# Rotary sums on all partitions, and the heads' blocks laid side by side by ScalarE copies, in a two-layer hybrid encoder step

## What is computed

```
hn = rmsnorm(x); proj = hn @ w_in
def rotary(x, pos):            # x: (B, L, heads, 64)
    x1, x2 = x[..., :32], x[..., 32:]
    return concatenate([x1 * cos - x2 * sin, x1 * sin + x2 * cos], axis=-1)
qa = rotary(heads(qa), pos)
ka = rotary(heads(ka), pos) * scale
A = retention(qa, ka, va)      # 4 heads, chunks of 64 frames
B = gated linear attention     # 4 heads, chunks of 64 frames
C = band attention             # 8 heads
x = x + concat[A, B, C] @ w_out
x = x + relu(rmsnorm(x) @ w_up)**2 @ w_down
```

## Time and profile before

| | |
|---|---|
| time before, median of 3 runs (from, to) | 1419.89 us (1417.8, 1420.12) |
| the profiled execution | 1420.84 us |
| its span, first to last instruction | 1419.0 us |
| granted TensorE clock, mean over the span | 0.991 |

### The profile page before, as it was taken

How to read it: one execution, slowest core, us unless ns; L and a number is a source line. 1 busy time by engine, 2 the same in 40 slices (tenths; PEclk the granted TensorE clock), 3 DMA queues, 4 the chain that set the end, 5 groups by cost and what they waited for, 6 DMA issues and landing times. The chain is left out here.

```text
span 1419.0 us, 28637 instructions
## 1 busy us (share of the span) xinstructions
PE 1386.3 (98%) x12590; PEld 1344.8 (95%) x12590; DVE 776.7 (55%) x1224; ACT 521.3 (37%) x859; POOL 147.1 (10%) x107
## 2 busy tenths in 40 slices
PE   8999999999999999999999999999999999999996
PEld 8899898899999999999998998989999999999996
DVE  6897767745434334344768967675453343433433
ACT  5333556633223223123433345565331231322331
POOL 0200000031110110200202000001301102002012
PEclk9999999999999999999999999999999999999997
DMA  6113333222222222222221224422222222222211
GB/s 230 61 65 100 95 118 95 78 102 90 88 81 87 89 90 90 90 90 89 77 75 46 67 88 132 134 74 77 88 90 90 90 90 90 85 82 88 89 61 63
DMA packets 50635, 127.82 MB, mean 90 GB/s; under 512 B 8400, under 2 KB 17744, under 8 KB 50512
## 3 DMA queue, kind: packets, MB, share of 16 engines
q1 hardware_dynamic: 50224, 125.44, 26.7%
q10 hardware_dynamic: 288, 0.55, 0.1%
HBM read 118.77 MB, written 7.21 MB: 89 GB/s over the span
## 5 line engine op out<-in xcount | busy, mean ns | idle before, releaser
L1302 PE MATMUL PS<-xhi,whi 128*128 128x272 f32 x1920 | 565.0, 294 | 4.0 <-DVE wlo L767 3.1
L1302 PE MATMUL PS<-xhi,wlo 128*128 128x272 f32 x1920 | 557.2, 290 | 0.0
L1302 PE MATMUL PS<-xlo,whi 128*128 128x272 f32 x1920 | 554.8, 289 | 0.0
L767 DVE TENSOR_TENSOR wlo<-raw,whi 128x1024 fp32r<-128x1024 f32 x200 | 252.9, 1264 | 386.1 <-ACT whi L467 385.3
L467 ACT ACTIVATE whi<-raw 128x1024 fp32r<-128x1024 f32 x200 | 211.5, 1059 | 548.4 <-PE PS L1302 543.9
L1302 PEld LDWEIGHTS PS<-xhi,whi 128*128 128x128 f32 x1920 | 363.2, 189 | 15.5 <-issue 9.7
L1302 PE MATMUL PS<-zhi,wlo 128*128 128x272 f32 x1280 | 371.0, 290 | 0.0
L1302 PE MATMUL PS<-zhi,whi 128*128 128x272 f32 x1280 | 368.8, 288 | 0.4 <-DVE wlo L767 0.4
L1302 PE MATMUL PS<-zlo,whi 128*128 128x272 f32 x1280 | 368.7, 288 | 0.0
L1302 PEld LDWEIGHTS PS<-xlo,whi 128*128 128x128 f32 x1920 | 363.8, 189 | 0.2
L1302 PEld LDWEIGHTS PS<-xhi,wlo 128*128 128x128 f32 x1920 | 363.3, 189 | 0.0
(11 more groups left out here) (226 smaller groups left out, 1050.3 us busy)
## 6 DMA issues: line engine op xcount, KB each, us to landing
raw<-in_wu SPq DMA_DIRECT2D x199, 512.0 KB, 3.4
Bh<-in_bias SPq DMA_DIRECT2D x16, 256.0 KB, 4.1
h<-in_x SPq DMA_DIRECT2D x8, 272.0 KB, 6.1
out_k_t<-att_k SPq DMA_DIRECT2D x8, 272.0 KB, 4.4
out_y_t<-y SPq DMA_DIRECT2D x8, 272.0 KB, 2.7
kct<-in_ck SPq DMA_DIRECT2D x8, 256.0 KB, 3.1
cvb<-in_cv SPq DMA_DIRECT2D x8, 256.0 KB, 4.7
out_v_p<-vtk SPq DMA_DIRECT2D x8, 256.0 KB, 2.2
```

What stands on the lines that cost most here:

```text
L767: nc.vector.tensor_tensor(wlo[n % SPL][:, :], raw[n % RAW][:, :], f32(whi[n % SPL][:, :]), ALU.subtract).then_inc(sems["w_lo"], 1)
L1302: return nc.tensor.matmul(out, lhsT, rhs, start=start, stop=stop, skip_group_check=True)
```

## The change

`rotary` becomes two DVE operations on all 128 partitions: the difference goes to the tile `r2`, the sum to `ssum` (both are free at this time). They are announced on a new semaphore, `rot_sum`. A new step of ACT, `"apart"`, then copies four blocks of 32x544 at a time from `r2` and `ssum` to their places in `rk` or `rq`, and raises `rot_ready`. It stands at the end of the ACT steps of slots (8, 1), (9, 0), (10, 1) and (11, 0). DVE's sums of q wait for the copies of k (`rot_ready` 2), since they use the same two tiles. In a run this takes away 32 DVE operations of 32x544 and adds 8 of 128x544 and 32 ACT copies of 32x544. The semaphore's entries in the lists of counts and names are left out here.

```diff
--- before.py
+++ after.py
@@ -73,7 +73,9 @@
     _steps[(12, 0)] = _steps[(12, 0)] + [("gn", GLA)]
     _steps[(15, 0)] = [("gn", RET)]
 GN_PARTS = [(0, 8), (8, 20)]
-ROTARY = {(8, 0): (RK, 0), (8, 1): (RK, 1), (10, 0): (RQ, 0), (10, 1): (RQ, 1)}
+ROTARY = {(8, 0): RK, (10, 0): RQ}
+for _slot, _first, _g in (((8, 1), RK, 0), ((9, 0), RK, 1), ((10, 1), RQ, 0), ((11, 0), RQ, 1)):
+    ACT_STEPS[_slot] = ACT_STEPS.get(_slot, []) + [("apart", _first, _g)]
 for _u in range(4):
     _b = 16 + 3 * _u
     DVE_STEPS[(_b + 1, 0)] = [("norm", _u, 0), ("score", _u, 1)]
@@ -565,6 +567,18 @@
                                 nc.scalar.activation(oT[j][:, 0:TP], PS[:, M0 + g, :], ACT.Copy)
                                 ins = nc.scalar.activation(oT[j][:, TP:T], PS[:, M0 + 2, g * TS:(g + 1) * TS], ACT.Copy)
                                 ins.then_inc(sems["back_read"], 1)
+                        elif what == "apart":
+                            _, first, g = st
+                            dst, c = rk if first == RK else rq, slice(g * T, (g + 1) * T)
+                            if layer and first == RK:
+                                for s in range(2):
+                                    act.wait_ge(sems[f"stored{s}"], nth(f"stored{s}", 0))
+                            act.wait_ge(sems["rot_sum"], nth("rot_sum", 1 + (first == RQ)))
+                            for p in range(2):
+                                s32 = slice(32 * (2 * g + p), 32 * (2 * g + p) + 32)
+                                nc.scalar.activation(dst[64 * p:64 * p + 32, c], r2[s32, :], ACT.Copy)
+                                ins = nc.scalar.activation(dst[64 * p + 32:64 * p + 64, c], ssum[s32, :], ACT.Copy)
+                            ins.then_inc(sems["rot_ready"], 1)
                         elif what == "parts":
 
                             _, u, p = st
@@ -815,7 +829,7 @@
                             dve.wait_ge(sems["rstd_ready"], nth("rstd_ready", 1))
 
                         if n == RQ:
-                            dve.wait_ge(sems["rot_ready"], nth("rot_ready", 2))
+                            dve.wait_ge(sems["rot_sum"], nth("rot_sum", 1))
 
                         def out(dst, by):
                             return nc.vector.tensor_tensor(dst, src, by, ALU.mult)
@@ -849,20 +863,14 @@
                                       halves(rstd))
                         ins.then_inc(sems["unit_read"], 1)
 
-                    def rotary(first, g):
-
-                        dst = rk if first == RK else rq
-                        if layer and first == RK and g == 0:
-                            for s in range(2):
-                                dve.wait_ge(sems[f"stored{s}"], nth(f"stored{s}", 0))
+                    def rotary(first):
+
                         dve.wait_ge(sems["unit_read"], nth("unit_read", first + 2))
-                        c = slice(g * T, (g + 1) * T)
-                        for p in range(2):
-                            s32 = slice(32 * (2 * g + p), 32 * (2 * g + p) + 32)
-                            nc.vector.tensor_tensor(dst[64 * p:64 * p + 32, c], rot[0][s32, :], sq[0][s32, :], ALU.subtract)
-                            ins = nc.vector.tensor_tensor(dst[64 * p + 32:64 * p + 64, c], rot[1][s32, :],
-                                                          sq[1][s32, :], ALU.add)
-                        ins.then_inc(sems["rot_ready"], 1)
+                        if first == RQ:
+                            dve.wait_ge(sems["rot_ready"], nth("rot_ready", 2))
+                        nc.vector.tensor_tensor(r2[:, :], rot[0][:, :], sq[0][:, :], ALU.subtract)
+                        nc.vector.tensor_tensor(ssum[:, :], rot[1][:, :], sq[1][:, :], ALU.add) \
+                            .then_inc(sems["rot_sum"], 1)
 
                     def square_sums(a, b):
                         return nc.vector.reduce_sum(gst[0][:, a:b], osq[:, a * HD:b * HD].rearrange("p (a c) -> p a c", c=HD),
@@ -1156,7 +1164,7 @@
                         if half == 0 and not rest_first:
                             rest(n + 1)
                         if (n, half) in ROTARY:
-                            rotary(*ROTARY[(n, half)])
+                            rotary(ROTARY[(n, half)])
                         if half == 0 and n > GATE + 1:
                             gate_rest(n - GATE - 2)
                         if half == 1 and n > GATE:
```

More of the change, by code:

```diff
@@ L100 @@
     pe_out_s=2, outs_act=2, outs_dve=4, centred=2, gn_var=2, gn_act=6, gn_done=4, pe_back=2, back_read=4,
-    rot_ready=4, ret_scaled=2, o_cleared=1, s_cleared=1, part_hi=8, part_lo=8, pe_heads=4, heads_act=4,
+    rot_sum=2, rot_ready=4, ret_scaled=2, o_cleared=1, s_cleared=1, part_hi=8, part_lo=8, pe_heads=4, heads_act=4,
     pe_score=8, score_dve=32, max_ready=8, exp_done=8, norm_done=8, pe_score_s=4, score_s_dve=8, exp_s=4,
@@ L268, in hybrid_encoder @@
             "pe_out_s", "outs_act", "outs_dve", "centred", "gn_var", "gn_act", "gn_done",
-            "pe_back", "back_read", "rot_ready", "ret_scaled", "o_cleared", "s_cleared",
+            "pe_back", "back_read", "rot_sum", "rot_ready", "ret_scaled", "o_cleared", "s_cleared",
             "part_hi", "part_lo", "pe_heads", "heads_act", "pe_score", "score_dve", "max_ready", "exp_done", "norm_done",
```

## The result

The changed kernel takes 1430.26 us (median of 6 runs, 1429.86 to 1432.83) against 1419.25 (6 runs, 1417.8 to 1420.12): ratio 1.0079, 95% interval 1.0068 to 1.0091. That is slower by 11.0 us; the profiled execution took 1430.46, its span is 1428.3.

A forecast was written before the change was run, and what follows sets the result against it. PE, busy 98% of the span, was taken as the bound. Waits of 1.65 + 3.67 - 0.56 a layer give 9.5 us a run; with 4.4 for the clock, 1419.89 + 13.9 = 1433.8, forecast 1434 us, range 1427 to 1439.

The forecast's parts named there:

- DVE's relief: Slot (12, 0): without DVE's backlog, PE's wait for `rk` goes, -0.56 us a layer; DVE loses 17.5 us busy a run.
- The price of a copy: Each ACT copy of 32x544 takes 0.66 us without overlap, scaled from 64x512 copies; four take 2.64 us.
- The first wait: Slot (9, 1): k's first four copies delay ACT's `ktok`, so PE's product of `ktok` and `vtok` waits, +1.65 us a layer.
- The second wait: Slot (11, 1): q's copies in ACT's queue make PE's product of `rk` and `rq` wait, +3.67 us a layer.
- Their sum: PE's two new waits less the ended `rk` wait: 4.76 us a layer, 9.5 us a run.
- The clock: PE's clock falls after both waits of 3.67 us and one of two of 1.65: three dips of 1.47, 4.4 us.
- my own case: Both new PE waits as computed, with two to four clock dips: 1432.3 to 1435.3 us, own range 1431 to 1437; chance 0.60.
- the rival with hardly a dip: Both new PE waits come, but with no clock dip or one: 1429.4 to 1430.9 us; chance 0.13.
- The one that is not slower: ACT's copies fit its idle time and DVE's relief decides: only 0.56 us gained, twice, 1418.8 us; chance 0.05.

The follow-up runs named there:

- experiment 2: Changed kernel with all eight copies of k placed behind ACT's `ktok` copies; 1430.71 us, ratio 1.0073 to the kernel before.
- experiment 3: Changed kernel with q returned to eight short DVE operations a layer, k left as in the change; 1423.69 us, ratio 1.0024 to the kernel before.
- 5: Changed kernel with four more ACT copies of 32x544 into an unused tile, ahead of q's last four; 1437.85 us, ratio 1.0124 to the kernel before.
- 6: Changed kernel with k's copies behind `ktok` and q's first four between ACT's copies to `O` and its squares; 1425.90 us, ratio 1.0039.
- again: The changed kernel, unaltered, timed once more in four runs; 1432.28 us, ratio 1.0083 to the kernel before.
- 7: Changed kernel with all sixteen copies of a layer on GpSimd in place of ACT; 1416.90 us, ratio 0.9978 to the kernel before.
- 4: Changed kernel with k's copies behind `ktok` and q on short DVE operations; 1417.78 us, ratio 0.9987 to the kernel before.

## Why the prediction was right

- **DVE's relief, -0.56 a layer.** Right. The wait is gone, and without any copies 1.0 us was all that the run gained beside the clock. DVE's busy time fell by 16.1 us, not 17.5.
- **The price of a copy, 0.66.** Right: 0.65 to 0.66, starts 0.665 apart. The rows of 64x512 that also change partitions were the right ones to scale. The budget of 0.3 us plus 0.83 ns an element from the Trainium skill (ScalarE: Activation LUTs, Rules for kernel authors) gives 0.75 as an estimate, and the trace has 0.65. That is no contradiction: the page gives the 0.3 us for an instruction whose bias is a pointer operand, which I had passed over, and these copies name no bias.
- **The first wait, +1.65.** Measured 1.63 and 1.72. It is what experiment 2 removes, and what stands alone in experiment 3.
- **The second wait, +3.67.** Measured 3.77 twice. It grows by 0.66 a copy (5), shrinks when copies go to an idle place (6) and goes without q's copies (3).
- **Their sum, 9.5 a run.** Measured 3.35 + 7.54 - 1.12 = 9.8; span less clock says 9.1 (changed), 8.7 (again).
- **The clock, 3 x 1.47 = 4.4.** This term was mis-sized. The median moved by 11.0, which leaves 1.2 for it (12.3 and 2.5 in the repeat). A dip came behind both long waits, at 1.31 each and not 1.47, but none behind the waits of 1.65, where I had put one. The 1.31 is no constant: over the six waits of 3.77 in three profiles it was 1.6 in the mean. What dips elsewhere do is chance in a single profile, 3.1 us in this pair. With 2 x 1.31 the forecast would have been 1432, with 2 x 1.6 1433.
- **The number.** 1430.26 is 3.7 below the forecast, and outside the 1431 to 1437 that I gave my own case. It lies in the band of the rival with hardly a dip (1429.4 to 1430.9), though in the profile both dips at the long waits came; it was the dips elsewhere that were fewer. The repeat, 1432.28, lies in my case's band. Which band a median of this kernel falls into is thus partly luck; that the waits alone give 9 to 10 us is not.
- **The rivals.** The one that is not slower rested on a price of 0.25 us or less a copy, and the copies cost 0.65. But an engine with nothing else in its queue makes it true: on GpSimd the relief of DVE comes through (7).

## What to carry to other kernels

Before work moves to an engine with idle time, ask what stands behind it in that engine's queue and how long before its reader that was done: here the slack was 1.6 us ahead of one product and none ahead of the other (ACT's squares of the sample, which the last copies now stand behind, ended at 109.84 + 0.42 = 110.26, when PE had begun its product at 110.06), in an engine that is 37% busy. The relief of a full engine is worth the waits that it ends, not the busy time that it loses: here 16 us bought 1.1. The same copies cost nothing when they stand behind what is urgent (k, in 4), or on an engine whose queue is empty (GpSimd, in 7).

## What the runs showed that was not expected

- GpSimd copies a block of 32x544 in 0.64 us, as fast as ACT's 0.66, though its operation with one input and 128x544 took 1.18 in the kernel before.
- The clock does not follow from a wait's length alone: behind the waits of 1.8 us for `Ps` it fell in 10 of 26 cases over thirteen profiles, behind those of 1.65 for `ktok` in none of 8, behind those of 2.3 in one of 2. Why is open.
- The versions without the new waits lost less to the clock than the kernel before (7.6 to 9.3 us a run against 10.6 to 10.8), though only the 0.56 us waits for `rk` separate their lists of waits. That is part of their gain of 0.11 to 0.22%, and its cause was not found.
